# Two heads' scores back to back in an attention loop, with the dense work around it dealt out anew

## The reference, cut to what matters

```python
mh = head_layernorm(mlstm(...), mh_norm_g)                 # four heads of 256
ya = sigmoid(p["m_o"]) * mh * silu(p["m_z"])
# sparse attention: 8 heads of 64 in 2 groups, queries in 4 blocks of 128
kc = (gelu(blocks(n_kc) @ w1)) @ w2                        # 31 compressed keys; vc likewise
o_c = softmax(q_raw @ kc.T + mask) @ vc                    # the compressed branch
o_s = softmax(q_rope @ ks.T + causal) @ vs                 # at 512 tokens all 8 blocks are chosen
o_w = softmax(q_rope @ kw.T + causal) @ vw                 # the window is 512
yn = g0 * o_c + g1 * o_s + g2 * o_w
yb = yn * silu(p["n_z"])
merged = sigmoid(p["g_a"]) * (ya @ w_branch_a) + sigmoid(p["g_b"]) * (yb @ w_branch_b)
x = x + merged @ w_out
```

## Time and profile before

| | us |
|---|---|
| median of three runs | 2082.38 |
| the profiled execution | 2084.87 |
| its span in the trace | 2083.2 |
| TensorE busy in it | 1993.6 |
| VectorE busy | 995.2 |
| ScalarE busy | 793.2 |

### The profile page before, as it was taken

How to read it: one execution, slowest core, us unless ns; L and a number is a source line. 1 busy time by engine, 2 the same in 40 slices (tenths; PEclk the granted TensorE clock), 3 DMA queues, 4 the chain that set the end, 5 groups by cost and what they waited for, 6 DMA issues and landing times.

```text
span 2083.2 us, 25619 instructions
## 1 busy us (share of the span) xinstructions
PE 1993.6 (96%) x9406; PEld 1628.1 (78%) x9406; DVE 995.2 (48%) x1409; ACT 793.2 (38%) x1334; POOL 171.0 (8%) x192
## 2 busy tenths in 40 slices
PE   6999899999999999999999989999899999999998
PEld 5888778677778877888887777799688878888886
DVE  5688666543334444333333758634533343333332
ACT  3334333344432334343322654334422234434332
POOL 1101110000000020000001120023200010000010
PEclk9999999999999999999999999999999999999999
DMA  8967713111104423333333313220233423333331
GB/s 292 305 177 246 270 33 93 50 42 41 31 26 121 125 62 101 92 95 96 103 91 105 86 49 94 77 56 11 76 96 101 146 62 105 95 96 98 91 103 49
DMA packets 330628, 212.85 MB, mean 102 GB/s; under 512 B 21357, under 2 KB 315178, under 8 KB 330030
## 3 DMA queue, kind: packets, MB, share of 16 engines
q1 hardware_dynamic: 319024, 170.58, 28.2%
q0 software_dynamic: 10368, 37.75, 5.1%
q10 hardware_dynamic: 1150, 3.35, 0.4%
HBM read 204.31 MB, written 7.35 MB: 102 GB/s over the span
## 4 chain that ended last, share of the span: by engine, by line
PE 83%; DVE 9%; ACT 3%; issue 2%; DMA 2%; ACTq 1%; POOL 0%; SPq 0%; DVEq 0%; POOLq 0%
PE psum L431 23%; PE psum L433 23%; PE psum L432 23%; DVE delta_qkv_T L2005 2%; PE psum L1113 2%; PE psum L1137 1%; DMA ada_w<-in_ada_w 1%; PE psum L1321 1%; DVE w_lo L390 1%; DVE ada_sum L2005 1%; PE psum L1124 1%; PE psum L1000 1%; PE psum L888 1%; PE psum L1016 1%; PE psum L890 1%
## 5 line engine op out<-in xcount | busy, mean ns | idle before, releaser
L431 PE MATMUL psum<-act_hi,w_hi 128*128 128x512 f32 x1616 | 654.2, 405 | 14.6 <-ACT nsa_v_tokens L1417 5.8
L433 PE MATMUL psum<-act_hi,w_lo 128*128 128x512 f32 x1616 | 635.4, 393 | 0.0
L432 PE MATMUL psum<-act_lo,w_hi 128*128 128x512 f32 x1616 | 635.0, 393 | 0.0
L390 DVE TENSOR_TENSOR w_lo<-w_raw,w_hi 128x1024 fp32r<-128x1024 f32 x306 | 386.0, 1266 | 375.4 <-ACT w_hi L382 349.9
L382 ACT ACTIVATE w_hi<-w_raw 128x1024 fp32r<-128x1024 f32 x306 | 320.0, 1053 | 195.6 <-PE psum L433 182.9
L431 PEld LDWEIGHTS psum<-act_hi,w_hi 128*128 128x128 f32 x1616 | 307.5, 190 | 106.0 <-issue 36.4
L433 PEld LDWEIGHTS psum<-act_hi,w_lo 128*128 128x128 f32 x1616 | 306.4, 190 | 65.8
L432 PEld LDWEIGHTS psum<-act_lo,w_hi 128*128 128x128 f32 x1616 | 307.3, 190 | 61.5 <-issue 1.2
L713 POOL TENSOR_TENSOR squares<-squares 128x512 f32<-128x512 f32 x30 | 46.7, 1564 | 1310.7 <-ACT squares L1508 908.9
L431 PE MATMUL psum<-ffn_hi,w_hi 128*128 128x512 f32 x352 | 139.6, 396 | 0.0
L433 PE MATMUL psum<-ffn_hi,w_lo 128*128 128x512 f32 x352 | 139.0, 395 | 0.0
(11 more groups left out here) (347 smaller groups left out, 2420.5 us busy)
## 6 DMA issues: line engine op xcount, KB each, us to landing
w_raw<-in_ffn_w_in SPq DMA_DIRECT2D x88, 512.0 KB, 3.8
ada_w<-in_ada_w POOLq DMA_DIRECT2D x72, 512.0 KB, 5.7
w_raw<-in_w_in SPq DMA_DIRECT2D x68, 512.0 KB, 3.9
w_raw<-in_mix_w_in SPq DMA_DIRECT2D x52, 512.0 KB, 3.7
w_raw<-in_ffn_w_out SPq DMA_DIRECT2D x32, 512.0 KB, 3.8
w_raw<-in_ffn_w_out SPq DMA_DIRECT2D x16, 384.0 KB, 3.3
w_raw<-in_w_branch_a SPq DMA_DIRECT2D x8, 512.0 KB, 3.8
w_raw<-in_w_out SPq DMA_DIRECT2D x8, 512.0 KB, 3.8
```

What stands on the lines that cost most here:

```text
L390: dve.tensor_tensor(WLO[:, n % 4, :], RAW[:, n % 4, :], WHI[:, n % 4, :].bitcast(F32), ALU.subtract).then_inc(w_lo, 1)
L431: pe.matmul(out, whi, hhi, start=start, stop=False)
L432: pe.matmul(out, whi, hlo, start=False, stop=False)
L433: return pe.matmul(out, wlo, hhi, start=False, stop=stop)
```

## The change

1. Scores are issued in pairs (`score_pair`): an even and an odd head, one on each half of the rows, next to each other, in four banks (4, 5, 3, 0). A round now is a pair, with one dense quarter, and from pair 16 on with a second one between the two `turn` calls. The sums have one bank, 7, for all heads, so the first `apply_v` of a branch waits for `add_branch` of the one before.
2. The 112 quarters are dealt out anew: 48 instead of 64 in the loop, and 16 more in the compressed branch. `gate_tile` calls on ScalarE and VectorE move with them.
3. `VSW` moves to memory that is not shared with `ada_w`, with a number of other tiles that change place, and ScalarE's wait for the 72 sums goes.
4. The merge's first tiles come in the order g0, a0, g1, b0, a1, b1, with `y_back` between a0 and g1; `yb_hi` and `yb` take copies and splits by turns.

```diff
-        VSW = phase("nsa_v_tokens", 78, [NT, 2, P])
+        VSW = phase("nsa_v_tokens", 92.5, [NT, 2, P])
+        MERGE1 = [("g", 0), ("a", 0), ("g", 1), ("b", 0), ("a", 1), ("b", 1)] + [(x, f) for f in range(2, 8) for x in "gab"]
-        SCORE_BANK, NSA_PV_BANK, SIDE_BANK, SIDE_FROM = (4, 5, 3), (7, 0), (1, 2), 12
+        SCORE_BANK, SIDE_BANK, SIDE_FROM = (4, 5, 3, 0), (1, 2), 16
+        GATE_AT = {4: 16, 8: 17, 12: 18, 16: 19, 18: 20, 20: 21, 22: 22, 24: 23, 26: 24, 28: 25, 30: 26}
@@ TensorE, the compressed branch
-            oz(2)
+            oz(4)
             pe.wait_ge(sem("roped"), 2)
...
-            oz(2)
+            oz(4)
...
                 turn_h(f)
-                if f % 2:
-                    oz(1)
+                oz(1)
...
-            oz(8)
+            oz(16)
             pe.wait_ge(sem("cmp_probs"), 1)
@@ TensorE, the loop over units
+            def score_pair(p):
+                if p >= 2:
+                    pe.wait_ge(sem("exp_done"), 2 * p - 2)
+                elif p == 1:
+                    pe.wait_ge(bank_free[3], (Place("oz1", 0).tile + 14) // 4 + 1)
+                    pe.wait_ge(bank_free[0], (Place("oz1", 0).tile + 15) // 4 + 1)
+                for u in (2 * p, 2 * p + 1):
+                    i, g, b, hh = units[u]
+                    par = hh % 2
+                    r = slice(64 * par, 64 * par + 64)
+                    k = KVR[r, (2 + b + (0 if par == g else 2)) % 4, 0:(i + 1) * P]
+                    pe.matmul(PS[:, SCORE_BANK[u % 4], 0:(i + 1) * P], QROPE[r, 2 * g + hh // 2, i * P:i * P + P], k,
+                              start=True, stop=True).then_inc(sem("nsa_s"), 1)
...
-                if hh == 0 and u >= 8:
-                    pe.wait_ge(sem("y_added"), u // 4 - 1)
+                if hh == 0 and u:
+                    pe.wait_ge(sem("y_added"), u // 4)
...
-            for u in range(len(units) + 3):
-                if u < len(units):
-                    score(u)
-                if u < len(units):
-                    oz(1)
-                if 2 <= u < len(units) + 2:
-                    turn(u - 2)
-                if u >= 3:
-                    apply_v(u - 3)
+            for p in range(len(units) // 2):
+                score_pair(p)
+                oz(1)
+                if p:
+                    turn(2 * p - 2)
+                    if p > 1:
+                        apply_v(2 * p - 3)
+                    if p >= 16:
+                        oz(1)
+                    turn(2 * p - 1)
+                    apply_v(2 * p - 2)
@@ ScalarE
             tiles_ready(act, pl, 1)
-            act.wait_ge(sem("ada_used"), 8 * N_MOD)
             for t in range(NT):
                 tile_used(copy(VSW[:, t].rearrange("p a d -> p (a d)"), PS[:, pl.bank(t), 0:256]), pl, t)
...
-                if u % 4 == 0 and u:
-                    gate_tile(11 + u // 4)
-                if u in YA_AT:
-                    ya_hi(YA_AT[u])
+                p = u // 2
+                if u % 2 and p in GATE_AT:
+                    gate_tile(GATE_AT[p])
+                if u % 2 and p % 2 == 0 and 2 <= p <= 16:
+                    ya_hi(p // 2 - 1)
@@ VectorE: the compressed branch and the loop
-                if h == 1:
+                if h == 0:
                     gate_tile(7)
-            gate_tile(8)
+                elif h == 1:
+                    gate_tile(8)
+            gate_tile(9)
+            gate_tile(10)
             for i in range(NT):
                 dve.wait_ge(sem("cmp_s_sum"), i + 1)
...
+                if u % 2 == 0:
+                    continue
+                p = u // 2
+                if p % 2 and p >= 3:
+                    add_branch((p - 3) // 2)
+                if p in GATE_AT:
+                    gate_tile(GATE_AT[p])
+                if p % 2 and p <= 15:
+                    ya(p // 2)
+                if p % 2 and 3 <= p <= 17:
+                    ya_lo(p // 2 - 1)
```

More of the change, by code:

```diff
@@ L1792, in first_merge @@
                 pl = Place("merge1", 0)
-                for f in range(8):
-                    split_hi(act, pl, 3 * f + AHEAD)
-                    tiles_ready(act, pl, 3 * f)
-                    tile_used(act.activation(GT[:, f % 2, :], PS[:, pl.bank(3 * f), :], ACT.Tanh, scale=0.5), pl, 3 * f)
-                    split_hi(act, pl, 3 * f + 1 + AHEAD)
-                    if f == 0:
-                        yb_hi()
-                    split_hi(act, pl, 3 * f + 2 + AHEAD)
-                    act.wait_ge(product, UNITS["merge1"] + f + 1)
-                    act.activation(MGHI[:, f, :], OG[:, f, :], ACT.Copy, scale=0.5).then_inc(u_hi, 1)
+                for k, (kind, f) in enumerate(MERGE1):
+                    split_hi(act, pl, k + AHEAD)
+                    if k == 2:
+                        yb_hi()
+                    if kind == "g":
+                        tiles_ready(act, pl, k)
+                        tile_used(act.activation(GT[:, f % 2, :], PS[:, pl.bank(k), :], ACT.Tanh, scale=0.5), pl, k)
+                    elif kind == "b":
+                        act.wait_ge(product, UNITS["merge1"] + f + 1)
+                        act.activation(MGHI[:, f, :], OG[:, f, :], ACT.Copy, scale=0.5).then_inc(u_hi, 1)
             def ffn_in(name):
@@ L2406, in first_merge @@
                 pl = Place("merge1", 0)
-                for f in range(8):
+                for k, (kind, f) in enumerate(MERGE1):
                     a, b = OG[:, f, :], GT[:, f % 2, :]
-                    split_lo(dve, pl, 3 * f + AHEAD)
-                    split_lo(dve, pl, 3 * f + 1 + AHEAD)
-                    tiles_ready(dve, pl, 3 * f + 1)
-                    cnt.mark(stt(a, a, 1.0, PS[:, pl.bank(3 * f + 1), :], ALU.add, ALU.mult))
-                    if f == 0:
-                        yb()
-                    split_lo(dve, pl, 3 * f + 2 + AHEAD)
-                    tiles_ready(dve, pl, 3 * f + 2)
-                    chained(stt(b, b, 1.0, PS[:, pl.bank(3 * f + 2), :], ALU.add, ALU.mult))
-                    for q in (1, 2):
-                        dve.sem_inc(bank_free[pl.bank(3 * f + q)], 1)
-                    tt(a, a, b, ALU.add).then_inc(product, 1)
-                    dve.wait_ge(u_hi, UNITS["merge1"] + f + 1)
-                    stt(MGLO[:, f, :], a, 0.5, MGHI[:, f, :].bitcast(F32), ALU.mult, ALU.subtract).then_inc(u_lo, 1)
+                    split_lo(dve, pl, k + AHEAD)
+                    if k == 2:
+                        yb()
+                    if kind == "g":
+                        continue
+                    tiles_ready(dve, pl, k)
+                    g = a if kind == "a" else b
+                    chained(stt(g, g, 1.0, PS[:, pl.bank(k), :], ALU.add, ALU.mult))
+                    dve.sem_inc(bank_free[pl.bank(k)], 1)
+                    if kind == "b":
+                        tt(a, a, b, ALU.add).then_inc(product, 1)
+                        dve.wait_ge(u_hi, UNITS["merge1"] + f + 1)
+                        stt(MGLO[:, f, :], a, 0.5, MGHI[:, f, :].bitcast(F32), ALU.mult, ALU.subtract).then_inc(u_lo, 1)
             def residual(name, per_tile, gate_col):
```

134 lines of the change are left out of this document (62 added, 72 removed).

## The result

The changed kernel takes 2053.80 us in the median of 4 runs (2053.25 to 2060.54) against 2080.76 for the kernel before (4 runs, 2078.70 to 2084.11). The ratio is 0.9876, 95% interval 0.9851 to 0.9902: about 27 us less by the medians, where 30 were forecast. The profiled execution took 2053.66 us (span 2051.9), 31.2 less than the one before.

The account below looks back on a forecast made before the run. TensorE, busy 96% of the span, was taken as the bound, with time only in gaps, slow clock and matmul order. The terms -6.7 - 9.5 - 1.8 - 6.3 - 8.4 + 9.4 - 6.8 gave -30.1 us: 2052 us, range 2040 to 2067.

Parts of the forecast that it names:

- Value tiles: Before the mLSTM loop: TensorE's 5.8 us wait for ScalarE's value-tile copy mostly goes, with the slow clock behind; 6.7 us saved.
- Rival 5: Value-tile copy is held by something else, so its 6.7 us stay: 2059 us; on top of any other, no chance given.
- Compressed branch: In the compressed branch, 34 quarters instead of 18 cover TensorE's idle gaps and slow clock; 9.5 of 11.6 us saved.
- Quarters by themselves: Sixteen quarters moved out of the loop cost 1.40 us each in dense runs instead of 1.51; 1.8 us saved.
- Pairs: Loop scores: neighbours save 6.3 us of fixed cost, and one pass of four overlapping across halves saves 8.4 us more.
- Rival 3: Both passes of a pair's two scores run side by side, saving 8.4 us more: 2044 us; chance 0.08.
- The loop's own waits: First 16 pairs wait on single banks and gate tiles, with one slow stretch; 14.5 us against 5.1 before, 9.4 lost.
- the three holds: In pairs 4, 8 and 12 gate tiles delay the next maximum; 1.2 us of waiting each, 3.6 in all.
- Merge: At the merge, a gate tile covers TensorE's wait for yb's low parts, and the slow clock goes; 6.8 us saved.
- No overlap: The two halves do not overlap, so pairs save only the fixed part: 2061 us; chance 0.27.
- The starved loop: First 16 pairs wait every round on score, maximum and exponential; 25 us lost instead of 9.4: 2068 us; chance 0.16.
- Slower: Waits keep TensorE at 1.2 GHz throughout the first 16 pairs: +23 us, or 2105 us; chance 0.03.

Follow-up runs that it names:

- same_half: Changed kernel with heads taken in the order 0, 2, 1, 3, so both heads of a pair are on one half of the rows; 2075.65 us.
- between: Changed kernel with the single dense quarter of pairs 1 to 15 moved from behind the scores to between the two `turn` calls; 2041.86 us.
- early: Like between, but two quarters in each of the first 16 pairs and one in the last 16, gate tiles following; 2036.95 us.
- late_gate: Like between, but VectorE does gate tiles 16 to 18 one pair later than ScalarE; 2035.83 us.
- split_pair: Changed kernel with the round's first dense quarter put between the two scores of a pair instead of behind them; 2084.11 us.
- vsw_wait: Changed kernel with ScalarE's wait for the 72 sums put back before its copy of the value tiles, the tile staying in its new memory; 2060.68 us.
- merge_old: Changed kernel with the merge's tiles and `y_back` in the old order, copies and splits of yb still by turns; 2062.12 us.
- best: Like early, but VectorE's gate tiles of the first half come one pair later than ScalarE's; 2032.63 us.
- deal_back: Changed kernel with the 16 moved quarters back in the loop, two per pair, and the compressed branch covered as before; 2050.14 us.

## Why the prediction was right, and where it was not

**Value tiles**, -6.7 predicted, -7.2 in the traces, -6.9 by the run with the wait put back. Right, and the tile ahead of the products with the sums covers them, as was said. (The prediction read its length off the tile behind them, 255.87 to 261.45; the one ahead takes the same 5.60 us in the kernel after, 240.27 to 245.87.) Rival 5 is out.

**Compressed branch**, -9.5 predicted, -9.3 in the traces (57.7 us before plus 14 quarters of 1.40 is 77.3; it is 68.0; the other two of the 16 lie ahead of this window). The wait for the second pair of compressed scores stays, at 1.1 us, and one slow stretch of 3.4 us with it, 1.7 lost. Together that is 2.8 us where 2.1 were left for them. The first score comes 4.8 us later than before, where 6.2 was forecast; 1.1 of the difference was there before the value tiles.

**Quarters by themselves**, -1.8. Not measured apart; the sum below takes it as forecast.

**Pairs**, -6.3 - 8.4 = -14.7 predicted, -23.5 by the rows. This is the step that failed: "As each head's two passes come together in the queue (first, second, first, second) and TensorE starts matmuls in order, only the second pass of one head and the first of the other can lie side by side". The record shows the two first passes starting together, then the two second ones. Rival 3, given 0.08, is the mechanism. The high end of the bound, 16.8 us, was right, and same_half shows its rows: 1.91 us against 1.06. The Trainium skill (TensorE: Matmul & The Clock Gate, "Measured speedup vs the span model") says that tiles on different rows add some 4 ns each; the trace agrees but for a few ns, 1.06 us for two against 1.05 for one, 7 ns more. Its sentence on program order ("The mechanism"), which the prediction had set above it, speaks of matmuls and names no passes, and I had drawn from it an order of passes that no row showed.

**The loop's own waits**, +9.4 predicted, +16.3 measured. The term had two parts. The waits, 12.8 us forecast, came to 12.9, but that agreement is luck too: the three holds took 2.07, 2.12 and 1.76 us, just under 6 in all, where 1.2 each, 3.6, was forecast; a plain copy was waited for 0.29 us at 128 keys and 0.17 at 256 (0.4 and 0.3 forecast); the add 0.25 to 0.55 us in four rounds (1.0 and 0.85 in seven). The slow clock was mis-sized: one stretch of 1.7 us lost was forecast, and 17.0 us at half speed, 8.4 us lost, came. The prediction let one slow stretch stay, as in the earlier trace rows, for three holds. In the loop no wait is over 2.1 us, and the clock fell behind each of the three, after stretches that were busy for 72 to 81% in total. In between, early and late_gate less waiting went with less slow clock in the loop: 17.0 us in the changed kernel, then 6.8, none and none.

**Merge**, -6.8 predicted, -7.1 in the traces, -8.3 by the run with the old order, where the chain was longer by the same split.

**Sum.** In the traces -7.2 - 9.3 - 1.8 - 23.5 + 16.3 - 7.1 = -32.6, and outside these places -1.1 before 228 us and +2.5 behind the merge, where slow stretches fall elsewhere: -31.2. The -1.8 in it is the forecast's own. The forecast of -30.1 stands so close because 8.8 us too little on the pairs met 6.9 too little on the loop's loss. The time was right, the mechanism of the largest term was not, and a reader should weigh it so.

**Rivals.** No overlap (0.27) is refuted by same_half. The starved loop (0.16) is half there: what the short cover costs is 16 us, nearer to 9 than to the 25 of the bound. Its chain, from score through maximum and exponential, shows in the three holds; between shows that it is not late elsewhere, since with no quarter behind the scores only one wait of 1.0 us for the probabilities came. Slower (0.03): the clock did fall in the first 16 pairs, for 17 of the 71 us up to 466.5, and not throughout.

**What the parts don't add up to.** Each part undone by itself costs 6.9, 8.3, 30.3 and -3.7 us, 41.8 in total, against 27 that the change brings. split_pair has the largest excess, and it is slow clock that comes on top when the pair goes. Part of the excess may be chance: vsw_wait and merge_old have the changed kernel's loop, instruction for instruction, and yet 23.9 and 17.0 us of slow clock in it against 17.0, in stretches of other lengths. In these three traces each of the nine holds, of 1.8 to 2.1 us, has a slow stretch that starts 0.3 to 2.0 us behind it. In between the same holds have one for three, with the short waits gone, and in early, late_gate and best, where no wait is over 1 us, the loop has none. But what decides when the clock falls stays open: same_half and split_pair wait less in the loop than the changed kernel (9.4 and about 9 us against 12.9), have 14 and 10 us more of slow clock, and most of their stretches begin behind no hold.

## What to carry to other kernels

Put matmuls that use only half of the rows next to a neighbour of the other half, in another bank: here the second was free, and even on the same half the neighbour saved the fixed 0.2 us. When work is taken out of a loop, ask of each single buffer what lies between its reader and its next writer, and place what is left there: the same quarter in another place was worth 12 us. And when a loop gets many short waits with a longer one among them, look for slow clock beside the idle time: in the changed kernel 8.4 us were lost to it beside 12.9 us of waits. It is no fixed rate, since same_half lost some 15 beside 9.4 and deal_back 1.7 beside 5.7.

## What was not expected of the hardware

Two 64-row float32 matmuls of two passes each, on opposite halves, 64x512: 1.06 us, against 1.05 for one and 1.91 for two on the same half. The surplus over a single one is 7 ns at each of the four lengths, from 128 to 512 columns. Their first passes start together, then their second passes, so by their starts the passes of the two matmuls alternate. The ends of matmuls are modelled in the record; the duration of the pair rests on the start of the dense matmul behind it.

The clock falls to its lower level, 0.51, also where no single wait is longer than 2.1 us: three stretches of 3.4, 6.8 and 6.8 us in the changed kernel's loop, four of 17.1, 3.4, 6.8 and 3.4 us in same_half, none in early, with the same number and shapes of matmuls in all three. The changed kernel's three begin 0.4 to 1.2 us behind waits of 2.07, 2.12 and 1.76 us.
